# Seven block products instead of eight in two token groups of a SwiGLU layer, with summed weight blocks in DRAM

## Chip, cores and metric

One NeuronCore of one Trainium2 chip. The metric is the device time of one execution in microseconds; the time given for a kernel is the median of its runs.

## What is computed

One layer of a streaming encoder for 2048 prompt tokens and 32 sample tokens, width 1024: a pooling and stick-breaking attention mixer with its output product and norm, then a SwiGLU feed-forward with width 2816, residual and a second norm. The change is in the feed-forward. Cut to that:

```python
h = (layer_norm(x) * (1.0 + sc2) + sh2)
gu = h @ w_gu                                  # (tokens, 1024) @ (1024, 2 * 2816)
ff = (silu(gu[..., :D_FF]) * gu[..., D_FF:]) @ w_down   # (tokens, 2816) @ (2816, 1024)
x = layer_norm(alpha * x + g2 * ff, ln2_g, ln2_b)
```

## The kernel before

All large products run in float16 in three terms: each operand is split into a high and a low float16 half, scaled, and high x high, high x low and low x high are accumulated in float32 (`TERMS`). ScalarE writes the high half of a block, VectorE its low half (float32 block times scale minus high half).

**Tokens.** `hidden_t` holds the transposed input of the feed-forward, 128 partitions x 8 blocks of the width x 2 halves x 2080 tokens. The feed-forward runs in three groups of tokens (`grp`): group 0 is tokens 0 to 767 in two blocks of 384, group 1 tokens 768 to 1535 likewise, group 2 the last 544 in two blocks of 272.

**Gate and up.** For each group, 22 slabs `j` of 128 columns of the feed-forward width. `gate_up(grp, j)` on TensorE does, for each token block and for gate and up, 8 x 3 matmuls, 96 a slab (L2063); the banks are 0 and 1 for block 0, 2 and 3 for block 1. ScalarE takes the sigmoid of gate (L1059), VectorE multiplies twice (L1606, L1609) into `E_H`, ScalarE writes the high half of the result (L1061) and GpSimd the low half (`lo_hid`, L786) into `E_HID`, which keeps the group's whole hidden layer. The weights of a slab, 1 MB in float32, come through one raw buffer `E_GRAW` by two DMAs of SyncE (`load_gu`, L604), are split by ScalarE (`gu_split`, L1050) and VectorE (`gu_low`, L1571) into one of two buffers `E_GHL`, and are loaded and split anew in each of the three groups. SyncE issues the load of a block once the low part of the block before is written (`next_gu`).

**Down.** After the 22 slabs of a group come two passes over the 22 slabs of `w_down` (`down(p)`, L2103), each with the token tiles of `PASSES[p]` in four slots of two banks: three tiles a pass, but in the fifth pass (p = 4) two, tile 12 and the sample tokens (32 rows, which rotate over four row groups of the output), and in the sixth (p = 5) three. Slabs are loaded by ScalarE's queue (`load_dn`, L1067) into three raw buffers, split by ScalarE (`dn_split`, L1071) and VectorE (`dn_low`, L1615) into four homes; a home is free when TensorE has used the slab four before. The last six slabs of the last pass are gone through tile by tile. `summed` (L1632, L1636) multiplies a tile's result by the gate row and adds the residual, `counted` takes its statistics (L1149 to L1152) and `normed` (L1653, L1654) writes the norm; for the tiles of a group's first pass this happens in the first slabs of its second pass, for those of the second pass in the first slabs of the next group or at the end.

**The stage ahead** works tile by tile (17 tiles): TensorE's output product (L1998) and transposes (L1987), VectorE's `front_d` (L1536, L1540), `xhat_d` (L1550) and `back_d` (L1559, L1564), ScalarE's `tile_d` (L813, L821), GpSimd's `lo_d` (L770). The first two blocks of `w_gu` are loaded and split in this stage: block 0 after tile 9 on ScalarE and after tile 12 on VectorE, block 1 after tiles 12 and 15.

Each engine runs its instructions in the order written by hand; semaphores count operations.

Of the kernel before, what the change touches and what calls it, by code (L numbers as in the profile page):

```python
# [31 lines left out]
P = 128  # L32
D = 1024
KD = D // P
# [17 lines left out]
TOP = 14  # L52
# [5 lines left out]
def encoder_step(nc, x_prompt, x_sample, cache_k, cache_v, state_pool, c_prompt, c_sample,  # L58
# [5 lines left out]
    with ctx:  # L64
# [12 lines left out]
        x1_dram = nc.dram_tensor("x1_dram", (TOK, D), f32).ap()  # L77

# [13 lines left out]
        WORK = 33000  # L92
# [101 lines left out]
        E_GRAW = w32(22576, 2048).rearrange("p (k w n) -> p k w n", k=KD, w=2)  # L194
        E_GHL = [w16(24624 + 2048 * s, 4096).rearrange("p (h k w n) -> p h k w n", h=2, k=KD, w=2) for s in range(2)]
        E_DHL = [w16(at, 2048).rearrange("p (h n) -> p h n", h=2)
                 for at in (24624, 25648, 26672, 27696, 22576, 23600)]
        E_DRAW = [w32(28720 + 1024 * i, 1024) for i in range(3)]
# [9 lines left out]
        ct_mm, csig_set, ct_set = sem("ct_mm"), sem("csig_set"), sem("ct_set")  # L208
# [7 lines left out]
        hist_mm, hist_set = sem("hist_mm"), sem("hist_set")  # L216
# [24 lines left out]
        o_scaled, o_split, tri_set = sem("o_scaled"), sem("o_split"), sem("tri_set")  # L241
# [5 lines left out]
        g1_mm, g1_set = sem("g1_mm"), sem("g1_set")  # L247
# [12 lines left out]
        g2_mm, g2_set = sem("g2_mm"), sem("g2_set")  # L260
# [70 lines left out]
        def blk_cols(grp, blk):  # L331
            return E_BLKS[grp][blk][0] - E_BLKS[grp][0][0]

        LN2_TILES = [*range(13), NT, *range(13, NT)]
        PASSES = [((0, 2), (1, 3), (2, 0)), ((3, 1), (4, 2), (5, 3)), ((6, 2), (7, 3), (8, 0)),
                  ((9, 1), (10, 2), (11, 3)), ((12, 2), (13, 3)), ((14, 0), (15, 1), (16, 2))]
# [15 lines left out]
        def slab_home(g):  # L352
            return g % 4 if g < 6 * NF - 2 else 4 + g % 2
# [26 lines left out]
        def _(sp):  # L380
# [42 lines left out]
            sp.wait_ge(hist_mm, 1)  # L423
# [113 lines left out]
            sp.wait_ge(npool_out, 4)  # L537
# [63 lines left out]
            def load_gu(c):  # L601

                for w in range(2):
                    sp.dma_start(E_GRAW[:, :, w, :], w_gu_c[c, w]).then_inc(gu_raw, 16)  # L604
# [7 lines left out]
            for t in range(14):  # L612
                step_d(t, t % 2)
                if t == 8:
                    sp.wait_ge(so_split, 1)
                    load_gu(0)
                if t == 12:
                    sp.wait_ge(gu_lo, 1)
                    load_gu(1)
# [11 lines left out]
            def next_gu(c):  # L631
                sp.wait_ge(gu_lo, c)
                load_gu(c % NF)
# [18 lines left out]
            for grp in range(3):  # L652
                n0, g0 = 6 * grp, 2 * NF * grp
                for c in range(2 if grp == 0 else 1, NF):
                    next_gu(NF * grp + c)
                    if grp and 3 <= c < 6:
                        y_out(n0 - 3 + c - 3)
                    if 8 <= c < 11 and c - 8 < len(PASSES[2 * grp]):
# [5 lines left out]
                for j in range(NF):  # L664
                    if j in (8, 10, 13) and (8, 10, 13).index(j) < len(first):
                        y_out(first[(8, 10, 13).index(j)][0])
                    if j in (15, 17, 19):
                        x1_in(second[(15, 17, 19).index(j)][0])
                    if j == 11 and grp < 2:
                        next_gu(NF * (grp + 1))  # L670
            for n in (14, 15, 16):
# [5 lines left out]
        def _(pool):  # L677
# [33 lines left out]
            for t in range(NT + 1):  # L711
# [7 lines left out]
                               base=0, pattern=[[1, P]], channel_multiplier=-1).then_inc(tri_set, 1)  # L719
# [53 lines left out]

            for t in range(NT + 1):
# [3 lines left out]
                rstd_d(d_aggr2, d_rstd2, t + 1, t % 2)  # L778
            lo_d(15, 1)
# [8 lines left out]

            def rstd_e(n):
                pool.wait_ge(e_aggr, n + 1)  # L790
                rstd(E_STAT[n % 3]).then_inc(e_rstd, 1)

            for grp in range(3):
                for j in range(NF):
                    for blk in range(len(E_BLKS[grp])):
                        lo_hid(grp, j, blk)
                        if grp and j < 3 and blk == 0:
                            rstd_e(6 * grp - 3 + j)
                for n, slot in PASSES[2 * grp]:
# [5 lines left out]
        def _(act):  # L805

            act.wait_ge(ct_mm, 1)
            act.activation(A_CSIG, ps[:, 6, 0:16], ACT.Sigmoid).then_inc(csig_set, 1)
# [82 lines left out]
            for g in range(4):  # L891
                w_split(g + 1, (g + 1) % 2)
                if g:
                    act.wait_ge(pooled_set, g)
                    act.wait_ge(npool_mm, g)
# [149 lines left out]
            def gu_split(n, s, used):  # L1045
# [4 lines left out]
                act.activation(E_GHL[s][:, 0, :, :, :], E_GRAW, ACT.Identity, scale=c1(C_SGU)).then_inc(gu_hi, 1)  # L1050
# [11 lines left out]

            def load_dn(g):
# [3 lines left out]
                act.dma_start(E_DRAW[g % 3], w_down[0, P * j:P * (j + 1), :]).then_inc(wd_raw[g % 3], 16)  # L1067

            def dn_split(g):
                act.wait_ge(wd_raw[g % 3], 16 * (g // 3 + 1))  # L1070
                act.activation(E_DHL[slab_home(g)][:, 0, :], E_DRAW[g % 3], ACT.Identity,  # L1071
                               scale=c1(C_SWD)).then_inc(wd_hi, 1)
                if g and g + 2 < 6 * NF and g % (2 * NF) not in (2 * NF - 2, 2 * NF - 1):
                    load_dn(g + 2)

            def gate_rows(b):
                act.wait_ge(g2_mm, b + 1)
                act.activation(E_G2[:, b, :], ps[:, 4 + 2 * b:6 + 2 * b, :].rearrange("p a n -> p (a n)"),
                               ACT.Identity).then_inc(g2_set, 1)

            for t in range(15):
# [6 lines left out]
                if t in (9, 12):  # L1088
                    gu_split(t // 3 - 3, t // 3 - 3, None)

            for grp in range(3):
                g0 = 2 * NF * grp
                for j in range(NF):
                    if j == NF - 2:
                        for g in range(g0, g0 + (3 if grp == 0 else 2)):
                            load_dn(g)
                    if j == NF - 1:
                        act.wait_ge(gu_mm, hid_n(grp, NF - 1, 0) - 1)
                        dn_split(g0)
                        dn_split(g0 + 1)  # L1100
                    elif j:
                        gu_split(NF * grp + j + 1, (j + 1) % 2, hid_n(grp, j, 0) - 1)
                    elif grp:
# [1046 lines left out]
```

## Time and profile before

| what | value |
| --- | --- |
| time, median of 3 runs | 2651.2 us (2649.56 to 2651.84) |
| time of the profiled execution | 2656.61 us |
| its span from first to last instruction | 2654.9 us |
| TensorE matmul busy | 2501.5 us, 94% |
| VectorE, ScalarE, GpSimd busy | 1484.5 us, 1111.9 us, 642.4 us |
| mean granted TensorE clock | 0.98 |
| DMA traffic | 308.10 MB, mean 116 GB/s |

The profile is one execution. Its page gives the busy time of each engine, the chain of work that ended last (followed back from the last instruction to what released each step) and the costliest groups of instructions; the trace behind it can be asked for single instructions in order of time, for groups in a stretch, for DMA issues and for busy time by stretch. GpSimd's spans are rough. Matmuls are pipelined, so the time of one is read from how long a dense run of them lasts. In a row, `work`, `ps`, `hidden_t` are memory tensors (`ps` is PSUM), and "SPq", "ACTq" are DMA issues of the queues of SyncE and ScalarE.

### The profile page before, as it was taken

How to read it: one execution, taken by the hardware profiler on the slowest of the kernel's cores; microseconds unless marked ns; L12 is line 12 of the kernel's file. 1: busy time of each engine (PE TensorE's matmuls, PEld its weight loads, DVE VectorE, ACT ScalarE, POOL GpSimd, SP SyncE). 2: the span in 40 equal slices, each digit the busy share in tenths (PEclk: the TensorE clock that was granted, in tenths of full speed). 3: DMA queues.
4: the chain of work that ended last, by engine and by line, in shares of the span. 5: the costliest groups of instructions: out<-in, count | busy, mean ns of one | idle time of the engine just before them, and what ended most of it. 6: DMA issues, size and time to landing. Idle time of an engine off the chain costs nothing.

```text
span 2654.9 us, 36761 instructions
## 1 busy us (share of the span) xinstructions
PE 2501.5 (94%) x14856; PEld 1401.6 (53%) x14856; DVE 1484.5 (56%) x1795; ACT 1111.9 (42%) x1489; POOL 642.4 (24%) x843
## 2 busy tenths in 40 slices
PE   4899899899999889998999999999999999999988
PEld 3445455444444344555666654456666544888633
DVE  4648555588888887797332333553323354633465
ACT  2522232699999892234222232222222322333331
POOL 2300000477777782333111100011111000111000
PEclk7899999999999999999999999999999999999999
DMA  7215778332332113231222234522222344433463
GB/s 242 98 49 200 257 257 257 98 96 80 96 83 61 32 64 122 72 113 66 64 93 75 64 98 138 193 80 80 91 68 64 119 138 164 125 105 94 132 216 96
DMA packets 262530, 308.10 MB, mean 116 GB/s; under 512 B 27693, under 2 KB 221037, under 8 KB 256602
## 3 DMA queue, kind: packets, MB, share of 16 engines
q1 hardware_dynamic: 243354, 236.54, 28.3%
q10 hardware_dynamic: 19008, 69.21, 8.3%
q8 instruction: 118, 1.93, 0.3%
q14 instruction: 50, 0.41, 0.0%
HBM read 267.32 MB, written 38.40 MB: 115 GB/s over the span
## 4 chain that ended last, share of the span: by engine, by line
PE 61%; DVE 8%; ACT 4%; POOL 3%; issue 3%; DMA 1%; POOLq 0%; DVEq 0%; ACTq 0%
PE ps L2063 34%; PE ps L2103 16%; PE ps L1998 3%; DVE work L1402 3%; PE ps L1873 2%; POOL work L738 2%; PE ps L1850 2%; PE ps L1889 2%; ACT work L963 2%; ACT ps L975 2%; DMA work<-in_w_down 1%; DVE work L1559 1%; DVE work L1399 1%; DVE work L1149 0%; DVE work L1564 0%
## 5 line engine op out<-in xcount | busy, mean ns | idle before, releaser
L2063 PE MATMUL ps<-hidden_t,work 128*128 128x384 f16 (+1 forms) x6336 | 932.2, 311 | 0.6 <-DVE work L1609 0.6
L2063 PEld LDWEIGHTS ps<-hidden_t,work 128*128 128x128 f16 x6336 | 619.7, 98 | 312.4 <-issue 1.5
L2103 PE MATMUL ps<-work 128*128 128x512 f16 x2244 | 473.6, 381 | 9.7 <-DVE work L1615 5.9
L1757 PE MATMUL ps<-hidden_t,work 128*128 128x416 f16 x1920 | 354.9, 346 | 14.2 <-DVE hidden_t L1167 9.9
L2103 PEld LDWEIGHTS ps<-work 128*128 128x128 f16 x2244 | 207.6, 98 | 275.2 <-issue 27.7
L786 POOL TENSOR_TENSOR work<-work 128x384 f16<-128x384 f32 (+1 forms) x132 | 113.9, 863 | 925.1 <-ACT work L1061 925.1
L738 POOL TENSOR_TENSOR work<-work 128x512 f32<-128x512 f32 (+2 forms) x320 | 306.6, 964 | 111.8 <-DVE work L1402 62.9
L1606 DVE SCALAR_TENSOR_TENSOR work<-ps,col,work 128x384 f32<-128x384 f32 (+1 forms) x132 | 76.3, 578 | 437.5 <-ACT work L1059 437.5
L1615 DVE SCALAR_TENSOR_TENSOR work<-work,col 128x1024 f16<-128x1024 f32 x132 | 168.2, 1280 | 222.3 <-ACT work L1071 222.3
L1757 PEld LDWEIGHTS ps<-hidden_t,work 128*128 128x128 f16 x1920 | 190.6, 100 | 165.9 <-issue 19.7
L1059 ACT ACTIVATE work<-ps,col 128x384 f32<-128x384 f32 (+1 forms) x132 | 72.4, 549 | 479.6 <-PE ps L2063 479.6
L1071 ACT ACTIVATE work<-work,col 128x1024 f16<-128x1024 f32 x132 | 150.7, 1147 | 286.5 <-PE ps L2103 248.4
L1402 DVE TENSOR_TENSOR_SCAN work<-ps,work 128x512 f32<-128x512 f32 x192 | 237.4, 1271 | 34.7 <-ACT ps L975 33.7
L1571 DVE SCALAR_TENSOR_TENSOR work<-work,col 128x2048 f16<-128x2048 f32 x66 | 155.0, 2349 | 151.3 <-ACT work L1050 151.3
L1850 PE MATMUL ps<-work 128*128 128x512 f16 (+3 forms) x640 | 174.2, 355 | 37.6 <-DVE work L1402 30.0
L1873 PE MATMUL ps<-ident,work 128*128 128x128 f32 x1088 | 178.0, 280 | 21.6 <-POOL work L738 17.0
L1873 PEld LDWEIGHTS ps<-ident,work 128*128 128x128 f32 x1088 | 131.3, 143 | 88.8 <-DVE work L1420 28.4
L699 POOL TENSOR_TENSOR work<-work,col 128x1 f32<-128x1 f32 x68 | 40.6, 596 | 552.7 <-DVE work L1152 552.7
L963 ACT ACTIVATE work<-ps,col 128x1024 f32<-128x1024 f32 (+1 forms) x160 | 165.0, 1031 | 8.5 <-PE ps L1850 7.0
L975 ACT ACTIVATE ps<-ps,col 128x1024 f32<-128x1024 f32 (+1 forms) x160 | 161.4, 1009 | 2.1
L986 ACT ACTIVATE work<-ps,col 128x512 f32<-128x512 f32 (+2 forms) x240 | 148.2, 618 | 32.2 <-PE ps L1873 29.0
L1998 PE MATMUL ps<-work,hidden_t 128*128 128x512 f16 x720 | 160.2, 384 | 0.0
(216 smaller groups left out, 2164.5 us busy)
## 6 DMA issues: line engine op xcount, KB each, us to landing
work<-in_w_gu SPq DMA_DIRECT2D x132, 512.0 KB, 4.8
work<-in_w_down ACTq DMA_DIRECT2D x132, 512.0 KB, 3.6
work<-in_w_ada SPq DMA_DIRECT2D x24, 1024.0 KB, 5.3
work<-in_w_gu SPq DMA_DIRECT2D x22, 1024.0 KB, 5.7
work<-in_w_down SPq DMA_DIRECT2D x11, 1024.0 KB, 5.5
work<-in_x_prompt SPq DMA_DIRECT2D x8, 1024.0 KB, 7.0
work<-in_w_in SPq DMA_DIRECT2D x16, 512.0 KB, 6.6
out<-work SPq DMA_DIRECT2D x32, 256.0 KB, 5.6
```

The costliest lines, as they stand in the source:

```text
L738: pool.tensor_tensor(a[:, 0:n], a[:, 0:n], PRJ[:, j, BLK * kc + 1:BLK * kc + n + 1], ALU.mult).then_inc(prod_set, 1)
L963: act.activation(C_A[u % 3][:, j:j + 2, 0:n], ps[:, z:z + 2, 0:n], ACT.Sigmoid, scale=c1(C_Z + 2 * (h // 2) + 1)).then_inc(be_set, 1)
L975: act.activation(ps[:, z:z + 2, 0:n], ps[:, z:z + 2, 0:n], ACT.Sigmoid, scale=c1(C_Z + 2 * (h // 2))).then_inc(sg_set, 1)
L1402: v.tensor_tensor_scan(row, ps[:, m % 4, w - 1::-1], row, PRJ[:, j, at + w:at + w + 1], ALU.mult, ALU.bypass).then_inc(scan_set, 1)
L1571: v.scalar_tensor_tensor(E_GHL[s][:, 1, :, :, :].rearrange("p k w n -> p (k w n)"), E_GRAW.rearrange("p k w n -> p (k w n)"), c1(C_SGU), E ...
L1615: v.scalar_tensor_tensor(home[:, 1, :], E_DRAW[g % 3], c1(C_SWD), home[:, 0, :], ALU.mult, ALU.subtract).then_inc(wd_lo, 1)
L1757: mm = pe.matmul(ps[:, blk, 0:PB], B_HL[s][:, wh * KD * P + k * P:wh * KD * P + (k + 1) * P], hidden_t[:, k, xh, PB * blk:PB * (blk + 1)], ...
L1850: mm = pe.matmul(ps[:, m % 4, 0:w], C_Q[e][:, qt:qt + P], C_K[e][:, half, BLK * kc:BLK * kc + w], start=(half == 0), stop=(half == 1))
L1873: mm = pe.transpose(ps[:, 4 + k % 2, j * P:(j + 1) * P], C_A[u % 3][:, j, kt * P:(kt + 1) * P], ident[:, :])
L1998: mm = pe.matmul(ps[:, 2 * s + n, :], hidden_t[:, k, xh, tile_cols(t)], D_WO[k][:, wh, 512 * n:512 * (n + 1)], start=(k == 0 and (xh, wh) ...
L2063: mm = pe.matmul(ps[:, 2 * blk + w, 0:width], E_GHL[s][:, wh, k, w, :], hidden_t[:, k, xh, at:at + width], start=(k == 0 and (wh, xh) == ( ...
L2103: mm = pe.matmul(ps[r:r + rows, 2 * slot + half, :], E_HID[:, j, xh, at:at + rows], E_DHL[slab_home(g)][:, wh, 512 * half:512 * (half + 1) ...
```

## The change

For groups 1 and 2 the product of gate and up is written as a 2 x 2 block product: the width is halved (blocks 0 to 3 and 4 to 7), the tokens are halved (the two token blocks), and gate and up are the two column blocks. Seven products of half the width, with sums of weight blocks and sums of token blocks, give the four results (Strassen's scheme in Winograd's form). A product is 4 x 3 matmuls, a slab 84.

- In group 0 the old eight products stay. GpSimd computes four sums of weight blocks per slab from the raw buffer (`weight_sums`), ScalarE and VectorE split them (`sum_split`, `sum_low`) into `E_THL`, and SyncE stores them and three of the plain blocks to DRAM (`store_gs`, four DMAs, 1.79 MB a slab). The next block of `w_gu` is loaded only when the four sums are done. The first split waits until the stores of the slab before have landed.
- After group 0 and after group 1, GpSimd computes the four sums of token blocks (`token_sums`), each split into halves, over the columns of `hidden_t` that group 0 used.
- In groups 1 and 2 SyncE loads the seven ready pieces of a slab in three DMAs (`load_gs`) into one of two buffers; nothing is split there. TensorE runs the products in the order `GS_STEPS`: 2, 6, 5, 7, 1 of the next slab, 4, 3. Products 1, 6, 7, 4 accumulate in one bank, which ScalarE copies out after 1, 6 and 7; 2 has a bank, 5 and 3 share one. VectorE adds the copies and forms the hidden blocks.
- The passes of down are now 3, 3, 3, 3, 3 and 2 tiles: pass p = 4 takes tiles 12, 13 and the sample tokens, p = 5 tiles 14 and 15. The last two slabs of each group get homes of their own.
- The first block of `w_gu` is made low after tile 11, its sums are split after tiles 13 and 14 on ScalarE and after 14 and 15 on VectorE; block 1 is loaded after tile 13 and split in slab 0 of group 0.
- A scale exponent `TOP` goes from 14 to 12, and some semaphores are merged.

```diff
-        LN2_TILES = [*range(13), NT, *range(13, NT)]
-        PASSES = [((0, 2), (1, 3), (2, 0)), ((3, 1), (4, 2), (5, 3)), ((6, 2), (7, 3), (8, 0)),
-                  ((9, 1), (10, 2), (11, 3)), ((12, 2), (13, 3)), ((14, 0), (15, 1), (16, 2))]
+        LN2_TILES = [*range(14), NT, *range(14, NT)]
+        PASSES = [((0, 3), (1, 0), (2, 1)), ((3, 2), (4, 3), (5, 1)), ((6, 3), (7, 0), (8, 1)),
+                  ((9, 2), (10, 3), (11, 1)), ((12, 3), (13, 0), (14, 1)), ((15, 2), (16, 3))]
+        GS_STEPS = [(1, 0)] + [(q, j + (q == 1)) for j in range(NF) for q in (2, 6, 5, 7, 1, 4, 3)
+                               if (q, j) != (1, NF - 1)]
...
             def next_gu(c):
-                sp.wait_ge(gu_lo, c)
-                load_gu(c % NF)
+                sp.wait_ge(gu_lo, 5 * c - 4)
+                sp.wait_ge(t_sum, 4 * c)
+                load_gu(c)
+
+            def store_gs(n):
+                half = E_GHL[n % 2].rearrange("p h w k n -> p h (w k n)")
+                sp.wait_ge(gu_lo, 5 * n + 5)
+                if n:
+                    sp.wait_ge(gs_stored, 64 * n)
+                sp.dma_start(gs_dram[n, :, 0], half[:, :, 0:512]).then_inc(gs_stored, 16)
+                sp.dma_start(gs_dram[n, :, 1], half[:, :, 512:1024]).then_inc(gs_stored, 16)
+                sp.dma_start(gs_dram[n, :, 6], half[:, :, 1536:2048]).then_inc(gs_stored, 16)
+                sp.dma_start(gs_dram[n, :, 2:6], E_THL).then_inc(gs_stored, 16)
...
+                    elif c + 2 < NF:
+                        for q, first, last in ((2, 0, 2), (7, 2, 5), (3, 5, 7)):
+                            sp.wait_ge(gu_mm, product_n(grp, q, c))
+                            load_gs(c + 2, first, last)
...
+            def weight_sums(n, pair):
+                b11, b21, b12, b22 = [E_GRAW[:, 512 * i:512 * (i + 1)] for i in range(4)]
+                if pair == 0:
+                    pool.wait_ge(gu_raw, 32 * (n + 1))
+                    if n:
+                        pool.wait_ge(gu_lo, 5 * n)
+                    pool.tensor_tensor(E_TSUM[0], b12, b11, ALU.subtract).then_inc(t_sum, 1)
+                    pool.wait_ge(t_sum, 4 * n + 1)
+                    pool.tensor_tensor(E_TSUM[1], b22, E_TSUM[0], ALU.subtract).then_inc(t_sum, 1)
+                else:
+                    pool.wait_ge(t_sum, 4 * n + 2)
+                    pool.wait_ge(gu_lo, 5 * n + 2)
+                    pool.tensor_tensor(E_TSUM[0], b21, E_TSUM[1], ALU.subtract).then_inc(t_sum, 1)
+                    pool.wait_ge(t_sum, 4 * n + 3)
+                    pool.wait_ge(gu_lo, 5 * n + 3)
+                    pool.tensor_tensor(E_TSUM[1], b22, b12, ALU.subtract).then_inc(t_sum, 1)
...
+            def sum_split(n, pair):
+                for i in range(2 * pair, 2 * pair + 2):
+                    act.wait_ge(t_sum, 4 * n + i + 1)
+                    if n and i == 0:
+                        act.wait_ge(gs_stored, 64 * n)
+                    act.activation(E_THL[:, T_AT[i], 0, :], E_TSUM[i % 2], ACT.Identity,
+                                   scale=c1(C_SGU)).then_inc(gu_hi, 1)
...
+            for j in range(NF):
+                if j + 1 < NF:
+                    gu_split(j + 1, (j + 1) % 2, 2 * j if j else None)
...
+                hidden(0, j, 0)
...
+                    sum_split(j + 1, 0)
...
+                hidden(0, j, 1)
+                if j + 1 < NF:
+                    sum_split(j + 1, 1)
...
+                    if grp == 0:
+                        if j + 1 < NF:
+                            gu_low(j + 1, (j + 1) % 2)
+                        hidden(0, j, 0)
+                        if j + 1 < NF:
+                            sum_low(j + 1, 0)
...
+                        hidden(0, j, 1)
+                        if j + 1 < NF:
+                            sum_low(j + 1, 1)
...
+            def product(grp, q, j):
+                n, c0 = half_width(grp), E_BLKS[grp][0][0]
+                bank = 3 * (j % 2) + {1: 0, 6: 0, 7: 0, 4: 0, 2: 1, 5: 2, 3: 2}[q]
...
+                elif q in (6, 7, 4):
+                    pe.wait_ge(c_set, copy_n(grp, {6: 1, 7: 2, 4: 3}[q], j))
+                elif q == 3:
+                    pe.wait_ge(add_set, add_n(grp, 2, j))
...
+                for k in range(4):
+                    for wh, xh in TERMS:
+                        mm = pe.matmul(ps[:, bank, 0:n], E_GS[j % 2][:, GS_AT[q], wh, k, :],
+                                       hidden_t[:, k0 + k, xh, at:at + n],
+                                       start=(q in (1, 2, 5) and k == 0 and (wh, xh) == (0, 0)),
+                                       stop=(k == 3 and (wh, xh) == TERMS[-1]), skip_group_check=True)
+                mm.then_inc(gu_mm, 1)
```

## Rows read from the trace of the kernel before

**Rows 1.** The page's chain that ended last, by line, with shares of the span.
```profile
PE ps L2063 34%; PE ps L2103 16%; PE ps L1998 3%; DVE work L1402 3%; PE ps L1873 2%; POOL work L738 2%; PE ps L1850 2%; PE ps L1889 2%; ACT work L963 2%; ACT ps L975 2%; DMA work<-in_w_down 1%; DVE work L1559 1%; DVE work L1399 1%; DVE work L1149 0%; DVE work L1564 0%
```
**Rows 2.** The same chain in order of time: start us, us, what; feed-forward.
```profile
1242.17 15.76 PE ps L2063 x96
...
1258.81 15.60 PE ps L2063 x96
...
1571.68 170.94 PE ps L2103 x792
1742.62 343.20 PE ps L2063 x2112
...
2256.76 244.65 PE ps L2063 x2112
...
2566.29 77.90 PE ps L2103 x360
```
**Rows 3.** TensorE in order of time (start, us, instruction, idle before), fifth down pass.
```profile
2518.90 2.00 PE L2103 MATMUL ps<-work 128*128 128x512 f16 x12 [0.40 <-DVE work L1615]
2521.28 2.00 PE L2103 MATMUL ps<-work 128*128 128x512 f16 x12 [0.39 <-DVE work L1615]
```
**Rows 4.** DMA issues of 2500 to 2560 us: count, KB each, median us to landing.
```profile
work<-in_w_down ACTq DMA_DIRECT2D x24, 512.0 KB, 4.3
```
**Rows 5.** Groups of 1300 to 1560 us (group 0): shapes, count | busy us, mean ns | idle.
```profile
L1571 DVE SCALAR_TENSOR_TENSOR work<-work,col 128x2048 f16<-128x2048 f32 x16 | 37.6, 2351 | 40.8 <-ACT work L1050 40.8
L1050 ACT ACTIVATE work<-work,col 128x2048 f16<-128x2048 f32 x16 | 31.8, 1988 | 0.9 <-issue 0.9
L786 POOL TENSOR_TENSOR work<-work 128x384 f16<-128x384 f32 x34 | 31.0, 912 | 234.2 <-ACT work L1061 234.2
...
L1606 DVE SCALAR_TENSOR_TENSOR work<-ps,col,work 128x384 f32<-128x384 f32 x33 | 20.4, 618 | 137.1 <-ACT work L1059 137.1
L1059 ACT ACTIVATE work<-ps,col 128x384 f32<-128x384 f32 x33 | 19.1, 580 | 145.6 <-PE ps L2063 145.6
L1061 ACT ACTIVATE work<-work 128x384 f16<-128x384 f32 x34 | 17.8, 523 | 45.4 <-DVE work L1609 45.4
```
**Rows 6.** The same view of 2260 to 2500 us (group 2).
```profile
L1059 ACT ACTIVATE work<-ps,col 128x272 f32<-128x272 f32 x43 | 20.9, 487 | 103.0 <-PE ps L2063 103.0
```
**Rows 7.** GpSimd in order of time, attention stage, five operations back to back.
```profile
706.52 5.28 POOL L738 TENSOR_TENSOR work<-work 128x511 f32<-128x511 f32 x5
```
**Rows 8.** All engines in order of time, 1212 to 1218 us, the stage ahead.
```profile
1212.37 1.17 DVE L1536 TENSOR_TENSOR work<-ps,work 128x1024 f32<-128x1024 f32 x1
...
1212.67 1.06 ACT L821 ACTIVATE hidden_t<-work 128x1024 f16<-128x1024 f32 x1
...
1217.70 2.13 POOL L770 TENSOR_TENSOR hidden_t<-work,hidden_t 128x1024 f16<-128x1024 f32 x1
1217.77 3.14 DVE L1559 SCALAR_TENSOR_TENSOR work<-work 128x1024 f32<-128x1024 f32 x1 [0.71 <-POOL work L701]
```
**Rows 9.** The page's group of the low parts of the down slabs.
```profile
L1615 DVE SCALAR_TENSOR_TENSOR work<-work,col 128x1024 f16<-128x1024 f32 x132 | 168.2, 1280 | 222.3 <-ACT work L1071 222.3
```
**Rows 10.** SyncE's queue in order of time: the issue of one block of w_gu.
```profile
1313.27 0.99 SPq L604 DMA_DIRECT2D work<-in_w_gu  x2
```
**Rows 11.** Busy time by stretches after it; last come clock, DMA share, GB/s.
```profile
1316.20:1317.20 1.00, 1.00 (x8) 0.59 (x6) 0.01 (x1) 0.52 (x1) 0.36 (x1) 1.00 1.15 346
1317.20:1318.20 1.00, 1.00 (x9) 0.60 (x7) 0.00 (x0) 0.00 (x0) 0.55 (x1) 1.00 0.82 245
```
**Rows 12.** VectorE in order of time, 2557 to 2566 us, the row work of a tile.
```profile
2557.39 1.23 DVE L1636 SCALAR_TENSOR_TENSOR work<-work 128x1024 f32<-128x1024 f32 x1
...
2561.05 0.69 DVE L1149 BATCH_NORM_STATS2 work<-work 128x6 f32<-128x512 f32 x1
...
2564.44 1.29 DVE L1653 SCALAR_TENSOR_TENSOR work<-work,ln_rows 128x1024 f32<-128x1024 f32 x1 [0.71 <-POOL work L701]
```
**Rows 13.** The x1 stores (L610, 512 KB each): min, median, max to landing.
```profile
DMA to landing us min/median/max: 2.6/2.6/3.2
```

## What the change does to the time, predicted

> **What bounds the kernel now.** I read the page's chain of work first [rows 1]: half of the span is TensorE at two lines, L2063 (gate and up) and L2103 (down). The chain in order of time [rows 2] then shows these stages without a gap: a slab of gate and up in group 0 is 96 matmuls in 15.60 us, group 1 is 2112 matmuls in 343.20 us (162.5 ns each), group 2 is 2112 in 244.65 us (115.8 ns), two down passes of three full tiles are 792 in 170.94 us (215.8 ns). So a matmul taken out of these stages is time taken out, as long as nothing else ends later. The exception is the fifth down pass (two tiles a slab): its 12 matmuls take 2.00 us, but a slab comes only every 2.4 us, because the chain runs through the slab loads of 4.3 us [rows 3, 4]. From the end of group 2 (2256.76 + 244.65 = 2501.4) to the last matmul (2566.29 + 77.90 = 2644.2) passes 5 and 6 take 142.8 us.
>
> **Groups 1 and 2: seven products.** A slab has 7 x 4 x 3 = 84 matmuls instead of 96, so 22 x 12 = 264 go in each group: 264 x 0.1625 = 42.9 us and 264 x 0.1158 = 30.6 us [rows 2], all on the path. What is added lies on other engines. A product lasts 12 x 0.1625 = 1.95 us (1.39 us in group 2). Product 6 continues the bank of product 1 once ScalarE has copied it, 7 that of 6, 4 that of 7; the written order puts at least one other product between. A copy from PSUM is 0.58 us (0.49 us for 272 columns [rows 5, 6]) behind at most one sigmoid of that size: in group 2 the sigmoid ends some 1.0 to 1.1 us before product 7 needs copy 2, which takes half of that. ScalarE has 7 such operations a slab (about 3.4 us of 9.7), VectorE 7 (3.5 us), so both are in time; I cost this at nothing. Only the last slab has no product between 7 and 4: 0.1 + 0.58, plus product 3 waiting a moment in group 2: 0.75 and 0.8 us. Net: -42.1 and -29.8.
>
> The ready pieces come from DRAM, 1.79 MB a slab, in three DMAs. The tight one is the last piece of 512 KB: issued at the end of product 3, needed four products later, 5.6 us in group 2. A slab load of that size and row length takes 4.3 us with another in flight [rows 4]. Cost nothing; if it lands 1 us late in each slab, 22 us. At the turn from down to group 1 or 2 the pieces of slab 0 follow the freeing of homes 0 and 1, two slabs of 3.9 us before the end; 1.28 MB at 346 GB/s is 3.7 us plus 1.3 us of start. Nothing. The token sums are 64 GpSimd operations of about 0.9 us [rows 5], some 60 to 75 us in the 171 us of two down passes, and only slab 42 of 44 waits for them. Nothing.
>
> **Group 0: weight sums.** Here PE's work stays, but the one raw buffer is now held until GpSimd has read it four times. The trace has no operation on 512 columns of these kinds on ScalarE or VectorE; between 384 and 2048 columns [rows 5] they come to 0.64 and 0.75 us (between 0.52 and 1.99, and 0.62 and 2.35, for the widths on either side). A GpSimd sum is 5.28 / 5 = 1.06 to 1.09 us [rows 7]. One more thing decides: GpSimd and VectorE exclude each other when both read two SBUF inputs. L1559 takes 3.14 us beside the GpSimd subtraction of 2.13 us that began just before it [rows 8], while the same width alone takes 1.28 [rows 9]. The order written out makes a ring, counted from the end of VectorE's low part of a block (0): two hidden products to 1.30; ScalarE's high half to 1.85; its split of sum 0 to 2.5; the low part of sum 0 waits for GpSimd's hidden subtraction (to 2.85), ends 3.6; that of sum 1 to 4.35; then sum 2 to 5.45; sum 3 to 6.6; SyncE issues the next load, which takes 4.9 us (issued 1313.27, its traffic fading within the slice from 1317.2 [rows 10, 11]) to 11.55; GpSimd's sums 0 and 1 run to 13.9, beside ScalarE's split of 1.99; VectorE's low part of 2.35 waits for them and ends at **16.25 us**. That is more than PE's 15.60, so PE waits 0.65 us a slab. From slab 2 on that is 19 x 0.65 = 12.4 us. The stores are the second ring: they are issued at about 9.2, behind the load (to 11.3), and 1.79 MB at 346 GB/s end near 17; the next ring wants them at 16.25 + 1.8 = 18. Covered by 1 us, no more.
>
> By the Trainium skill, "SBUF — State Buffer", section "Who interferes with whom", a VectorE instruction with two SBUF inputs blocks against a GpSimd instruction that reads SBUF, and one with one SBUF input does not; the trace agrees, with the 3.14 us above. Without that rule the ring would be some 15 us and the 12.4 us would fall away.
>
> **Before slab 2.** In the stage ahead VectorE and the tile loop of TensorE are level. The first two sum splits stand behind ScalarE's tile 13, which ends at 1212.67 + 1.06 = 1213.7, and VectorE would go on at 1212.37 [rows 8]: 1213.7 + 0.64 + 1.5 is 1216.0, so +3.7; the port adds about 1; the second pair (1.5) replaces the low part of block 1 (2.3), -0.8, which moves behind the last normalisation and costs 2.35 there, some of it covered before. Slab 1 starts about 5 us late. The ring above, begun with sums 0 and 1 behind GpSimd's last tile, puts slab 2 at 1266.9 instead of 1258.8: **+8.1**, with the 0.87 us of turns now inside waits. Old end of group 0: 1571.7 [rows 2]; new: 1266.9 + 19 x 16.25 + 15.6 = 1591.3. **+19.6 us.** The DMA waits at the end of group 0 (slab 2 of down behind the last store) have two slabs of cover.
>
> **Down passes 5 and 6.** A full tile is 6 x 0.2158 = 1.295 us a slab; the sample tile is 2.00 - 1.295 = 0.70 [rows 3]. Pass 5 becomes 22 x (2.59 + 0.70) = 72.4 us, more than the supply of 2.4 us a slab; pass 6 22 x 2.59 = 57.0, also more. With the fold of the sample (1.9) that is 131.3. But the row work of three tiles now falls into the 2.59 us slabs: VectorE has per slab one low part (1.28) and alternately statistics (about 1.5, from 2 x 0.69 and the aggregate) or the norm (2 x 1.29), with sums of 2 x 1.23 at the start [rows 9, 12]. Laid out slab by slab from the end of pass 5 the low parts of slabs 6, 7 and 9 come 1.0, 1.2 and 1.2 us late: 3.4 us; the last slab's load 0.4. Together 135.1 instead of 142.8: **-7.7**. If the burst is fully hidden it is -11.5; if VectorE gates eight slabs at 3.9 us, -1.
>
> **Sum.** 19.6 - 42.1 - 29.8 - 7.7 = -60.0 us. Against the profiled span of 2654.9: 2594.9. The profiled execution took 2656.6, 5.4 us over the median 2651.2; I take the difference from the median: **2591 us**.
>
> **Rivals.** (1) Group 0 stays bound by PE: the ring is 15.6 or less, since GpSimd and VectorE happen to alternate. For it: the excess is only 0.65 us, and two of its terms are interpolated. Time: 2591 - 12.4 = 2579. (2) The ring is longer, 17.25 us: each GpSimd operation that meets the port later costs up to 1.1 us, the load meets stores of the slab before. For it: everything in the ring is in series, and the ring has ten hand-overs. Time: 2591 + 19 x 1.0 = 2610. (3) The copies gate the products: each of the three chained products of a slab waits 0.25 us more than thought, 44 x 3 x 0.25 = 33 us, 2624. Against it: 0.5 us of slack [rows 6]; for it: no row shows a bank that ScalarE must read between two products. It includes the case that the seven products don't save an eighth. (4) Slower than before: the stores set group 0. If 1.79 MB go out at half the rate, 174 GB/s, they take 10.3 us instead of 5.2; the ring from the store's issue is 2.2 (behind the load) + 10.3 + 0.5, and 7.35 from the first split to the next issue: 20.3 us. Then +4.05 x 20 = 81: 2672. It decides from a ring of 19.2 us on, stores at about 190 GB/s. Against it: the x1 stores of 512 KB land in 2.6 us [rows 13], faster than any load.
>
> **How the numbers follow.** Forecast 0.50; (1) 0.14; (2) 0.20; (3) 0.09; (4) 0.05; the rest near no change 0.02. 0.2% is 5 us, about what a measurement of this kernel tells from none. Faster 0.93, same 0.02, slower 0.05. The range takes in (1) with 7 us for the bounds of passes 5 and 6 and of the first slabs, and (2) and (3): 2572 to 2626.
>
> **What would show it.** In the chain, group 1 should last near 302 us and group 2 near 216; each sum of waits of L2063's successor in them under 3 us. Slabs of group 0 should start every 16.2 us, with PE waiting on VectorE's block low part or its hidden product, and the releaser of ScalarE's block split should be the w_gu load. Pass 5 should be dense at 72 us, pass 6 should show PE waiting for L1615's successor in slabs 5 to 10. I am wrong if the sum splits wait for a store (rival 4), or if products wait for ScalarE's copies (rival 3).

## The result and the profile after

The changed kernel takes **2626.1 us** (2623.55 to 2626.38, 4 runs) against 2651.5 us for the one before in the same comparison: ratio 0.9897, 95% interval 0.9885 to 0.9908. It is faster, as forecast, but by 25 us instead of 60, and 0.1 us outside the range of 2572 to 2626. The profiled execution has a span of 2624.2 us against 2654.9.

The chain of the kernel after, in order of time (start, us, what), the lines that answer to [rows 2]. L2362 is the old product in group 0, L2393 the new one, L2431 down, L1916 the sum of a down tile:
```profile
1592.12 18.61 PE ps L2362 x96
1610.73 81.60 PE ps L2431 x378
...
1699.90 1.24 DVE work L1916
1701.18 83.05 PE ps L2431 x384
1784.24 296.41 PE ps L2393 x1824
2081.22 4.07 PE ps L2393 x24
2085.29 81.60 PE ps L2431 x378
...
2265.16 205.91 PE ps L2393 x1776
2471.54 2.95 PE ps L2393 x24
2474.49 67.96 PE ps L2431 x376
...
2604.23 9.24 PE ps L2431 x42
```
TensorE in order of time (start, us, instruction, idle before it), slabs 1, 2, 3 and some later ones of group 0:
```profile
1242.17 17.81 PE L2362 MATMUL ps<-hidden_t,work 128*128 128x384 f16 x96 [2.85 <-DVE work L1856]
...
1264.37 18.65 PE L2362 MATMUL ps<-hidden_t,work 128*128 128x384 f16 x96 [3.51 <-DVE work L1856]
...
1283.72 15.76 PE L2362 MATMUL ps<-hidden_t,work 128*128 128x384 f16 x96
1299.88 15.76 PE L2362 MATMUL ps<-hidden_t,work 128*128 128x384 f16 x96 [0.39 <-DVE work L1856]
...
1351.51 33.04 PE L2362 MATMUL ps<-hidden_t,work 128*128 128x384 f16 x192 [2.57 <-DVE work L1856]
1384.83 15.76 PE L2362 MATMUL ps<-hidden_t,work 128*128 128x384 f16 x96 [0.28 <-DVE work L1856]
...
1472.36 15.76 PE L2362 MATMUL ps<-hidden_t,work 128*128 128x384 f16 x96 [0.95 <-DVE work L1856]
1489.01 15.76 PE L2362 MATMUL ps<-hidden_t,work 128*128 128x384 f16 x96 [0.89 <-DVE work L1856]
```
From such lines, stage by stage, profile against profile (us; "forecast" is the prediction's own term):

| stage | before | after | change | forecast |
| --- | --- | --- | --- | --- |
| start to slab 1 of group 0 | 1242.2 | 1242.2 | 0.0 | +5.0 |
| slab 1 to slab 2 | 16.6 | 22.2 | +5.6 | +3.1 |
| slab 2 to the end of group 0 | 312.9 | 346.4 | **+33.5** | +11.5 |
| down passes 1 and 2 | 170.9 | 173.5 | +2.6 | 0 |
| group 1, gate and up | 343.2 | 301.1 | -42.1 | -42.1 |
| down passes 3 and 4 | 170.9 | 173.5 | +2.6 | 0 |
| group 2, gate and up | 244.6 | 215.7 | -29.0 | -29.8 |
| down passes 5 and 6 | 142.8 | 139.0 | **-3.8** | -7.7 |
| sum | | | -30.7 | -60.0 |

So the seven products gave what they should, and more than half of it went back in group 0. The first row hides something: slab 1 starts at the same time in both profiles, but in the changed kernel TensorE waits 8.1 us instead of 4.7 for the normalised tile 14 and 2.9 instead of 0.6 before slab 1, and spends 0.9 us less in between. That is 4.8 us more, which the earlier start of the rest of this one execution covers; the profiles of kernels with the changed code reach slab 1 at 1241.2 to 1246.6 us, those of the two with the old code at 1237.9 and 1242.2. With 4.8 in the first row the sum is -25.9; the medians are 25.4 us apart.

The experiments were timed against further runs of the kernel before, with medians of 2653.1 us (7 runs, for the first four) and 2654.0 us (15 runs, for the others). Totals of different experiments can therefore be off against each other by a few us, and the terms below go by stages of the profiles.

### The profile page after: what moved, and what is told of

It is laid out like the page before. It is cut to its first block, busy times and chain, and to the rows that moved or that the text cites. A ratio compares the mean times of both kernels' runs of the same rounds, so it can differ in the third digit from the quotient of the medians.

```text
span 2624.2 us, 36708 instructions
## 1 busy us (share of the span) xinstructions
PE 2438.6 (93%) x14328; PEld 1348.7 (51%) x14328; DVE 1556.5 (59%) x1971; ACT 1143.1 (44%) x1665; POOL 896.2 (34%) x1061
## 4 chain that ended last, share of the span: by engine, by line
PE 49%; DVE 9%; ACT 6%; issue 5%; DMA 5%; POOL 5%; SPq 1%; POOLq 0%; DVEq 0%; ACTq 0%
PE ps L2393 19%; PE ps L2431 15%; PE ps L2297 6%; DVE work L1642 3%; DMA work<-in_w_gu 3%; PE ps L2172 2%; POOL work L812 2%; PE ps L2149 2%; PE ps L2188 2%; DMA gs_dram<-work 2%; ACT work L1111 2%; ACT ps L1123 2%; ACT work L1199 1%; POOL work L860 1%; DVE work L1818 1%
## 5 line engine op out<-in xcount | busy, mean ns | idle before, releaser
L2393 PE MATMUL ps<-hidden_t,work 128*128 128x384 f16 (+1 forms) x3696 | 515.2, 303 | 1.9 <-ACT work L1242 1.1
L2431 PE MATMUL ps<-work 128*128 128x512 f16 x2244 | 472.5, 380 | 12.2 <-DVE work L1899 7.4
L2393 PEld LDWEIGHTS ps<-hidden_t,work 128*128 128x128 f16 x3696 | 361.4, 98 | 155.7 <-ACT work L1242 1.8
L2362 PE MATMUL ps<-hidden_t,work 128*128 128x384 f16 x2112 | 356.2, 332 | 29.6 <-DVE work L1856 29.6
L2431 PEld LDWEIGHTS ps<-work 128*128 128x128 f16 x2244 | 206.5, 98 | 277.7 <-issue 28.7
L1899 DVE SCALAR_TENSOR_TENSOR work<-work,col 128x1024 f16<-128x1024 f32 x132 | 178.4, 1357 | 207.0 <-ACT work L1273 207.0
L2362 PEld LDWEIGHTS ps<-hidden_t,work 128*128 128x128 f16 x2112 | 208.3, 99 | 177.0 <-issue 47.0
L2056 PEld LDWEIGHTS ps<-hidden_t,work 128*128 128x128 f16 x1920 | 189.6, 99 | 161.5 <-issue 15.5
L888 POOL TENSOR_TENSOR work<-work 128x384 f16<-128x384 f32 (+1 forms) x88 | 75.2, 859 | 418.1 <-ACT work L1262 418.1
L2172 PE MATMUL ps<-ident,work 128*128 128x128 f32 x1088 | 177.9, 280 | 21.9 <-POOL work L812 17.1
L2188 PE MATMUL ps<-work 128*64 128x512 f32 (+3 forms) x640 | 160.3, 557 | 0.0
```

The costliest lines, as they stand in the source:

```text
L2056: mm = pe.matmul(ps[:, blk, 0:PB], B_HL[s][:, wh * KD * P + k * P:wh * KD * P + (k + 1) * P], hidden_t[:, k, xh, PB * blk:PB * (blk + 1)], ...
L2172: mm = pe.transpose(ps[:, 4 + k % 2, j * P:(j + 1) * P], C_A[u % 3][:, j, kt * P:(kt + 1) * P], ident[:, :])
L2188: pe.matmul(ps[r:r + HD, 6 + b % 2, j0:BLK], C_V[e][:, 4 * kc + kt, :], C_AT[k % 4][:, j0:BLK], start=(kc == b and kt < 2), stop=(kc == 0 ...
L2362: mm = pe.matmul(ps[:, 2 * blk + w, 0:width], E_GHL[s][:, wh, w, k, :], hidden_t[:, k, xh, at:at + width], start=(k == 0 and (wh, xh) == ( ...
L2393: mm = pe.matmul(ps[:, bank, 0:n], E_GS[j % 2][:, GS_AT[q], wh, k, :], hidden_t[:, k0 + k, xh, at:at + n], start=(q in (1, 2, 5) and k == ...
L2431: mm = pe.matmul(ps[r:r + rows, 2 * slot + half, :], E_HID[:, j, xh, at:at + rows], E_DHL[slab_home(g)][:, wh, 512 * half:512 * (half + 1) ...
```

## Experiments

**A second raw buffer in group 0.** Slab n's block of `w_gu` goes to one of two raw buffers from slab 2 on; the second lies where two x1 tiles will come, and their loads move behind the 22 slabs.
```diff
+        E_GRAW2 = w32(16896, 2048)
+        def raw_of(n):
+            return E_GRAW if n < 2 or n % 2 else E_GRAW2
...
             def next_gu(c):
-                sp.wait_ge(gu_lo, 5 * c - 4)
-                sp.wait_ge(t_sum, 4 * c)
+                sp.wait_ge(gu_raw, 32 * c)
+                if c > 2:
+                    sp.wait_ge(gu_lo, 5 * (c - 2) + 1)
+                    sp.wait_ge(t_sum, 4 * (c - 1))
                 load_gu(c)
...
-                        store_gs(c)
                         if c + 2 < NF:
                             next_gu(c + 2)
+                        store_gs(c)
```


> The changed kernel with a second raw buffer for w_gu in group 0 (in the space of two x1 tiles, whose loads move behind the 22 slabs), so that the next block is loaded a slab earlier. Theory (ring): in the changed kernel a slab of group 0 takes 16.65 us or more because the one raw buffer is released only after the fourth weight sum, and load, split, sums and low parts follow in series; with two buffers slabs start every 15.6 us and slab 2 starts some 4 us earlier: 2626 - 19 x 1.65 - 3 = about 2592 us. Rival (engines full): VectorE and GpSimd, which exclude each other at the shared port, have no room for the added work in 15.6 us; then a second buffer leaves the slabs near 16.6 us: 2617 us or more. Rival (stores): the 1.79 MB of stores a slab set the pace, then no change, 2626.

Measured: 2592.0 us, ratio to before 0.9767 (0.9750 to 0.9783). TensorE in order of time in that kernel:
```profile
1263.48 15.76 PE L2371 MATMUL ps<-hidden_t,work 128*128 128x384 f16 x96
...
1279.95 296.56 PE L2371 MATMUL ps<-hidden_t,work 128*128 128x384 f16 x1824
```
Slab 1 still began late, after 2.9 us of waiting, at 1245.4; from slab 2 on the group is one dense run of 15.6 us a slab, as before the change, with every sum, split and store still in it. The work added was never too much for the engines; the ring through the one raw buffer was the cost. That settles against the rival of full engines, and the rival of the stores: ScalarE now does wait for stores before 20 of the first sum splits, 46.4 us in all, and none of it reaches TensorE. The edit also moves the x1 loads and puts each load ahead of the stores of the slab before; the run with the x1 loads alone moved, below, gives a small part of this gain, and no run has the new order of loads and stores alone.

**Stores of one slab only.** The stores of slabs 1 to 21 are left out, every wait for a store asks for slab 0's alone, and groups 1 and 2 read slab 0's pieces each time, so it computes something else.
```diff
                 sp.wait_ge(gu_lo, 5 * n + 5)
                 if n:
-                    sp.wait_ge(gs_stored, 64 * n)
+                    return
...
-                             gs_dram[j, :, first:last]).then_inc(gs_in[j % 2], 16)
+                             gs_dram[0, :, first:last]).then_inc(gs_in[j % 2], 16)
```


> The changed kernel with the stores of slab 0 alone; groups 1 and 2 read the pieces of slab 0 for every slab, so the output is not the reference's. Sums, splits and loads are as before. Ring theory: the plain slabs stay at 16.65 us, and only the six slabs that are longer (17.1 to 18.9 us) fall to it, since the stores lengthen a load (7.0 instead of 4.9 us) or hold a split: 2626 - 9 = 2617 us. Rival (stores): group 0 falls to 15.6 us a slab, 2587 us.

Measured: 2617.7 us, ratio 0.9862 (0.9847 to 0.9877). Slabs in the middle of group 0:
```profile
1467.33 15.76 PE L2362 MATMUL ps<-hidden_t,work 128*128 128x384 f16 x96 [0.93 <-DVE work L1856]
1483.94 15.76 PE L2362 MATMUL ps<-hidden_t,work 128*128 128x384 f16 x96 [0.85 <-DVE work L1856]
1500.61 15.76 PE L2362 MATMUL ps<-hidden_t,work 128*128 128x384 f16 x96 [0.91 <-DVE work L1856]
```
The slabs start every 16.6 us without any store. The slabs of 17.1 to 18.4 us in the changed kernel are gone; only the last interval is still 18.3 us (1567.0 to 1585.3). The stores cost about 8 us in all by way of single slabs, the ring the rest.

**Sums on 8 columns.** Everything is issued and waited for as before, but the four sums, their splits and low parts work on 8 columns of 512; it computes something else.
```diff
-                b11, b21, b12, b22 = [E_GRAW[:, 512 * i:512 * (i + 1)] for i in range(4)]
+                b11, b21, b12, b22 = [E_GRAW[:, 512 * i:512 * i + 8] for i in range(4)]
...
-                    act.activation(E_THL[:, T_AT[i], 0, :], E_TSUM[i % 2], ACT.Identity,
+                    act.activation(E_THL[:, T_AT[i], 0, 0:8], E_TSUM[i % 2][:, 0:8], ACT.Identity,
```


> The changed kernel with the weight sums, their splits and low parts on 8 columns instead of 512 (one zero fill ahead), so the output is not the reference's; every wait, load and store stays. Ring theory: sums 2 and 3 (2.95 us), a split (0.7), two low parts (1.6) and the sums ahead of the low part of the block shrink to some 0.15 us each, the ring is below 15.6 us and TensorE's 29.6 us of waits for VectorE go, store waits too for the most part: 2626 - 30 = 2596 us. Rival (stores): 2620 us or more.

Measured: 2589.7 us, ratio 0.9759 (0.9744 to 0.9774). From slab 3 on one dense run again:
```profile
1277.52 296.56 PE L2364 MATMUL ps<-hidden_t,work 128*128 128x384 f16 x1824
```
The same single buffer, loads and stores, with shorter links, no longer hold TensorE: what counts is the length of the ring. It gained 36 us where 30 were expected. The expectation counted TensorE's waits alone; the matmuls at the lower clock that followed four of them (9.5 us of TensorE's time, told of below) are gone too, but for slab 1, which still waits 2.9 us and takes 18.4.

**The x1 loads moved.** From slabs 8 to 10 of group 0 to behind slab 21, nothing else.
```diff
-                    if 8 <= c < 11:
-                        if grp == 0 and c == 8:
-                            sp.wait_ge(d_x1, NT + 1)
-                            sp.wait_ge(gu_mm, 1)
+                    if grp and 8 <= c < 11:
                         x1_in(n0 + c - 8)
+                if grp == 0:
+                    sp.wait_ge(d_x1, NT + 1)
+                    sp.wait_ge(gu_mm, 1)
+                    for n in range(3):
+                        x1_in(n)
```


> The changed kernel with only the three x1 loads of group 0 (512 KB each, issued in slabs 8 to 10) moved behind the 22 slabs. If they are what lets the stores reach into the next ring there, the slabs of 17.15, 17.69, 17.56 and 18.42 us fall to 16.65: 4 us less, 2622 us. If it is chance of the DMA engines: no change.

Measured: 2620.2 us (2620.0 to 2623.3), ratio 0.9878 (0.9864 to 0.9893). The four slabs beside which the loads had run (9 to 12) take 67.6 us together instead of 70.8, which is the expected direction, 3.2 us; but a slab of 17.6 us stands elsewhere in the group. In the changed kernel the first sum split of three slabs waits 0.7 us for stores that had been issued behind an x1 load, and here none does; but with the rows spread, below, the x1 loads stand where they were and none waits either. How the stores meet the loads differs from execution to execution, and this run alone does not settle the x1 loads' share.

**Slots 0 and 1 exchanged in passes 1 and 3.**
```diff
-        PASSES = [((0, 3), (1, 0), (2, 1)), ((3, 2), (4, 3), (5, 1)), ((6, 3), (7, 0), (8, 1)),
+        PASSES = [((0, 3), (1, 1), (2, 0)), ((3, 2), (4, 3), (5, 1)), ((6, 3), (7, 1), (8, 0)),
```


> The changed kernel with slots 0 and 1 exchanged in the first passes of groups 0 and 1 (third tile in slot 0, second in slot 1). In the changed kernel each second pass of these groups waits 2.4 us at its third tile, whose slot 1 held the third, last summed tile of the pass before (4.8 us in all, which the prediction left out). Theory: the slot now holds the second tile, summed 2.5 us earlier, so both waits go; at the end of group 0 the second tile waits up to 1 us for slab 21's second block: 2626 - 4 = 2622 us, and 0 to 1 us of waits for the gate product at these two places. Rival: VectorE's sums are late anyway and the wait moves to the start of group 1: 2626 or more.

Measured: 2617.1 us, ratio 0.9860 (0.9846 to 0.9874). The two waits of 2.4 us for L1916 are gone; passes 3 and 4 are one run of the old length:
```profile
1605.38 169.82 PE ps L2431 x786
...
2076.25 170.95 PE ps L2431 x792
```
At the end of group 0 the second tile waits 0.7 us, as expected. The stages give 4 to 5 us; that the whole kernel is 9 us below the changed one goes with a shorter group 0, which the edit does not touch (it ends 7 us earlier in this profile), so only the stages count here.

**Row work spread over every other slab of the last pass.**
```diff
-                    if 3 <= j < 3 + 2 * len(first):
+                    if grp == 2:
+                        if 3 <= j < 15 and j % 2:
+                            (counted, normed)[(j - 3) // 2 % 2](first[(j - 3) // 4])
+                    elif 3 <= j < 3 + 2 * len(first):
                         (counted, normed)[(j - 3) % 2](first[(j - 3) // 2])
-                    if grp == 2 and j == 5:
+                    if grp == 2 and j == 8:
                         summed(first[2])
```


> The changed kernel with the row work of the three tiles in the last pass put in every other slab (slabs 3 to 13, the sample's sum in slab 8) in place of every slab from 3 on. Theory: VectorE with a low part (1.28 us) and up to 2.6 us of row work in a slab of 2.59 us is late three times, 4.1 us of waits in slabs 5 to 10; spread, these fall to under 1 us: 2626 - 3.5 = 2622.5 us. The waits in the last six slabs (3.3 us) stay, since the slab loads set them. Rival (supply): the loads are late all through the pass, and the waits only move: 2626.

Measured: 2618.4 us, ratio 0.9865 (0.9852 to 0.9879). TensorE in the last pass, first of the changed kernel, then of this one:
```profile
2557.89 5.35 PE L2431 MATMUL ps<-work 128*128 128x512 f16 x24
2564.66 2.75 PE L2431 MATMUL ps<-work 128*128 128x512 f16 x12 [1.41 <-DVE work L1899]
2568.37 5.34 PE L2431 MATMUL ps<-work 128*128 128x512 f16 x24 [0.96 <-DVE work L1899]
2575.43 21.16 PE L2431 MATMUL ps<-work 128*128 128x512 f16 x96 [1.72 <-DVE work L1899]
2597.39 1.46 PE L2431 MATMUL ps<-work 128*128 128x512 f16 x6 [0.80 <-DVE work L1899]
2599.60 1.46 PE L2431 MATMUL ps<-work 128*128 128x512 f16 x6 [0.76 <-DVE work L1899]
```
```profile
2558.15 35.28 PE L2434 MATMUL ps<-work 128*128 128x512 f16 x162
2594.35 1.46 PE L2434 MATMUL ps<-work 128*128 128x512 f16 x6 [0.93 <-DVE work L1899]
2596.82 1.46 PE L2434 MATMUL ps<-work 128*128 128x512 f16 x6 [1.01 <-DVE work L1899]
```
The three waits of 4.1 us in the middle are gone, and the waits among the last six slabs stay (2.4 us, 3.3 before). Passes 5 and 6 take 133.3 us instead of 139.0 (2474.8 to 2608.0). So the middle was the row work, as laid out; the end is the supply: the first tile uses up the last six slabs at 1.3 us each, while ScalarE waits for each load. In the changed kernel:
```profile
2594.78 1.15 ACT L1273 ACTIVATE work<-work,col 128x1024 f16<-128x1024 f32 x1 [1.46 <-DMA work<-in_w_down]
...
2596.99 1.15 ACT L1273 ACTIVATE work<-work,col 128x1024 f16<-128x1024 f32 x1 [1.06 <-DMA work<-in_w_down]
```

**The passes alone, on the kernel before.** The last two passes of 3 and 2 tiles, nothing else.
```diff
-        LN2_TILES = [*range(13), NT, *range(13, NT)]
+        LN2_TILES = [*range(14), NT, *range(14, NT)]
...
-                  ((9, 1), (10, 2), (11, 3)), ((12, 2), (13, 3)), ((14, 0), (15, 1), (16, 2))]
+                  ((9, 1), (10, 2), (11, 3)), ((12, 2), (13, 3), (14, 0)), ((15, 1), (16, 2))]
```


> The kernel before with the last two passes of 3 and 2 tiles (12, 13 and the sample; 14, 15) and nothing else of the change. The prediction said 7.7 us less for this part; in the changed kernel's trace the stretch from the end of group 2 to the last matmul is 3.8 us shorter. Theory: the same 3.8 us less here, so about 2649 against 2653, the gain of the dense fifth pass (53 for 22 slabs of two tiles) given back in the sixth by the row work (4.1 us) and the last six slabs (3.3 us). Rival: the loss there belongs to the rest of the change; then 7 to 8 us less, 2645.

Measured: 2649.4 us, 4.6 us less; ratio 0.9985 (0.9977 to 0.9994). Its passes 5 and 6 run from 2498.8 to 2636.7, 137.9 us against 142.8. The part is worth 4 to 5 us wherever it stands, not 7.7.

**Second buffer, slots and spreading together.**

> The changed kernel with the second raw buffer, the exchanged slots and the spread row work together. If the three causes lie on different stretches, their gains add: 2592 - 4 - 3.5 = 2584.5 us. If one hides another, 2588 to 2592.

Measured: **2579.4 us** (2578.9 to 2580.0), ratio 0.9721 (0.9707 to 0.9734), 47 us faster than the changed kernel. The gains add within a few us; the whole is some 5 us better than expected. Its chain is the one wished for:
```profile
1276.01 296.41 PE ps L2374 x1824
...
1574.39 169.82 PE ps L2443 x786
1744.21 296.41 PE ps L2405 x1824
```

## Why the prediction was wrong

**Groups 1 and 2: right.** -42.1 and -29.0 us against -42.1 and -29.8. The copies of ScalarE between products are hidden, as costed; in both groups together TensorE waits 1.9 us for ScalarE. Rival (3) did not come.

**The ring in group 0: right mechanism, a mis-sized term.** Group 0 from slab 2 on took 22.0 us more than forecast, most of the error of 34 (60.0 against 25.9). The first step that failed is "SyncE issues the next load, which takes 4.9 us". One turn of the ring in the changed kernel, from the end of one low part (1471.04) to the end of the next (1487.69):
```profile
1468.26 2.78 DVE L1811 SCALAR_TENSOR_TENSOR work<-work,col 128x2048 f16<-128x2048 f32 x1 [5.42 <-ACT work L1199]
...
1474.45 1.65 POOL L860 TENSOR_TENSOR work<-work 128x512 f32<-128x512 f32 x1 [0.69 <-DVE work L1818]
...
1476.18 1.27 POOL L863 TENSOR_TENSOR work<-work 128x512 f32<-128x512 f32 x1
...
1477.52 1.00 SPq L644 DMA_DIRECT2D work<-in_w_gu  x2
...
1482.86 2.00 ACT L1199 ACTIVATE work<-work,col 128x2048 f16<-128x2048 f32 x1 [4.66 <-DMA work<-in_w_gu]
...
1484.90 2.79 DVE L1811 SCALAR_TENSOR_TENSOR work<-work,col 128x2048 f16<-128x2048 f32 x1 [5.37 <-ACT work L1199]
```
| part of the ring | measured | forecast |
| --- | --- | --- |
| low part's end to the issue of the load | 6.5 | 6.6 |
| issue to the start of ScalarE's split | 5.3 | 4.95 |
| start of the split to the end of the low part | 4.8 | 4.7 |
| one turn | 16.65 | 16.25 |

I had read the load's length off the traffic before; what counts is the time from its issue to the first instruction that uses it, 5.2 to 5.5 us in the plain slabs, and as long without stores (5.2 to 5.6 in the run without them). Single terms were also off, but cancelled: a free GpSimd sum is 1.27 us, not 1.09, sum 2 (L860) 1.65, and the block's low part 2.78 instead of 2.35, while it starts straight after the split, in the middle of a sum, instead of behind both. That they cancelled is luck. The turn is 0.4 us longer than forecast, 19 x 0.4 = 7.6 us.

**"Covered by 1 us, no more": the cover failed in single slabs; the main error.** Beyond 16.65 us the 19 intervals hold another 11.4 us, all of it in the ring. About 9 us lie between issue and split, above all in three slabs where it took 7.0 to 7.6 us and one of 6.4. I had the load first in the queue; the trace shows it shared: after a load issued at 1338.3 and stores issued from 1340.4 the block was ready only at 1345.4. Without the stores only the last slab's took long, 7.0 us; why that one, no run shows. Another 2.1 us are three first sum splits that waited for the stores of the slab before, the sign that I had named for rival (4), though 0.7 us each and not its price:
```profile
1403.10 1.33 ACT L1207 ACTIVATE work<-work,col 128x512 f16<-128x512 f32 x2 [0.70 <-DMA gs_dram<-work]
```
Together the slabs average (1592.1 - 1264.4) / 19 = 17.25 us, the value of rival (2). Of its two reasons "the load meets stores of the slab before" is the one that came; meetings at the port cost 0.4 us each, not "up to 1.1".

**A cost that the sum lacked: the clock.** TensorE's waits of about 3 us for VectorE were followed by slow matmuls. Busy time by stretches of the kernel after (us of the stretch, then PE, PEld, DVE, ACT, POOL; then granted clock, DMA share, GB/s):
```profile
1260.00:1264.00 4.00, 0.85 (x8) 0.61 (x6) 3.43 (x3) 0.91 (x2) 0.89 (x1) 0.93 0.49 207
1264.00:1268.00 4.00, 3.63 (x12) 1.75 (x13) 2.76 (x5) 2.21 (x4) 2.46 (x2) 0.50 0.01 4
1268.00:1272.00 4.00, 4.00 (x20) 2.05 (x18) 2.33 (x3) 2.77 (x4) 2.24 (x3) 0.72 0.24 66
1272.00:1276.00 4.00, 4.00 (x26) 2.41 (x25) 0.00 (x0) 0.98 (x1) 0.93 (x1) 1.00 1.11 356
```
TensorE stood for 3.5 us, then ran at 0.50, the lower of its two levels (1.2 of 2.4 GHz), and did 12 and 20 matmuls in stretches that hold 26. Slab 2 took 18.65 us instead of 15.76, slab 1 17.81, the last 18.61, slabs 7 and 8 together 1.7 us more: 9.5 us of TensorE's time. But only the last slab's 3.0 us (18.61 against 15.60) lengthened the kernel. Elsewhere the ring set the next start, and the slow matmuls only shortened TensorE's next wait: slabs 7 to 9 are 33.3 us apart, two plain turns, and in the run without stores slab 2 was slow as well, yet slabs 2 to 5 are 49.96 us apart, three plain turns:
```profile
1267.47 17.44 PE L2362 MATMUL ps<-hidden_t,work 128*128 128x384 f16 x96 [3.90 <-DVE work L1856]
...
1285.62 31.36 PE L2362 MATMUL ps<-hidden_t,work 128*128 128x384 f16 x192
1317.43 15.76 PE L2362 MATMUL ps<-hidden_t,work 128*128 128x384 f16 x96 [0.45 <-DVE work L1856]
```
So the 22.0 us are 7.6 of plain turns, 11.4 of loads and stores, and 3.0 of clock.

**The stage ahead and slab 1: about right** (+4.8 us by the waits, forecast +5). Slab 2 came 22.2 us after slab 1 instead of 19.7. It is not the slow slab 1: TensorE was through at 1260.9 and waited 3.5 us. The chain runs through the four sums behind GpSimd's last tile (from 1245.9), the load issued at 1252.9, ScalarE's split from 1258.4 and VectorE's low part. Which of these exceeds the forecast stays open, since that had only their total.

**Down passes 1 to 4: a step left out.** I costed no wait there. The third tile of passes 2 and 4 takes the slot that the last summed tile of the pass before had held, where the old rotation gave it the second's: 2.4 us twice, gone with the slots exchanged.

**Down passes 5 and 6: half.** "The low parts come 1.0, 1.2 and 1.2 us late: 3.4 us": measured 1.4, 1.0 and 1.7, 4.1. "The last slab's load 0.4" failed: four waits, 3.3 us, since the whole tail needs a slab every 1.3 us where loads give one in over 2. In the old pass of three tiles (3.9 us a slab) the tail had no wait [rows 2], presumably because the supply had run ahead; no run shows that lead by itself.

## What to carry to other kernels

A buffer that gains a reader lengthens the path from its release to its next filling: add up everything in series from one release to the next, the load from its issue to the first instruction that uses it, and ask for a second buffer when the sum comes within a tenth of the period. The four sums' work fitted easily; moving the x1 loads away made room for a second buffer, and the two together gave back 34 us. A slow stretch of TensorE costs time only where TensorE itself sets the pace. Where an accumulator slot is re-used, follow the rotation tile by tile, and where stall-free supply is needed at the end of a pass, count the supply at the rate of the tail.

## What the hardware showed

In the kernel after, waits of TensorE of 2.57, 2.85, 3.16 and 3.51 us in an otherwise dense run were followed by about 4 us or more at or near granted clock 0.50, each making its slabs 1.7 to 2.9 us longer; one of 2.66 us was not (slab 13 took 15.76 us), and those of 0.9 us never. The length of the wait alone does not tell: in the run with the rows spread a wait of 2.30 us was followed by a slab of 17.39 us, and waits of 2.25 and 2.28 us by slabs of 15.76; with the x1 loads moved, one of 2.51 us by 15.76. Nor does it take a long one: in the old code (the run with the passes) slab 1 was slow after waits of 1.33 and 0.59 us, with a granted clock of 0.70 from 1240 to 1244:
```profile
1237.91 17.44 PE L2063 MATMUL ps<-hidden_t,work 128*128 128x384 f16 x96 [0.59 <-DVE work L1609]
```
By the Trainium skill, "SBUF — State Buffer", section "Who interferes with whom", a VectorE instruction with two SBUF inputs and a GpSimd one that reads SBUF contend for a port pair, and the one that comes second blocks until the first is through. The trace fits: L860 and L1811 begin while the other engine is in such an instruction, and exceed their free durations here (1.27 and 2.35 us) by 0.38 and 0.43 us; GpSimd's spans are rough. Loads and stores of one queue did not follow one another: with stores issued 2 us behind a 1 MB load, the time from its issue to its use went from 5.3 to 7.0 us and more in some slabs and not in others, and without stores only in the last.
